# One slab earlier at the seam between attention heads and recurrent heads, and a loop turned by a stage

## What is computed

```
p = h @ w_in                       # q, k, v, z of 8 attention heads; qk, v, i, f, o, z of 4 recurrent heads
a = softmax(q1 k1) - lam * softmax(q2 k2);  o_a = a @ v
y_a = rmsnorm(o_a) * (1 - lam_init) * silu(z)
qk = silu(causal_dwconv(ml_qk))    # four taps over time, per channel
h = mlstm_chunkwise(q, k, v, i, f) # scores times decay, plus the carried state
y_b = rmsnorm(h * sigmoid(o)) * silu(z)
y = concat(y_a, y_b) @ w_out
```

## Time and profile before

| | |
|---|---|
| median of three runs | 2822.48 us (2818.57 to 2824.16) |
| span of the profiled execution | 2813.1 us |
| TensorE busy | 2699.3 us, 96% |
| VectorE, GpSimd, ScalarE busy | 1531.1, 1395.4, 1029.7 us |
| mean granted TensorE clock | 0.992 of 2.4 GHz |
| attention heads | about 862 to 1531 us |
| head norm and output of head 7 | about 1531 to 1557 us |
| first recurrent head | about 1557 to 1687 us |

### The profile page before, as it was taken

How to read it: one execution, slowest core, us unless ns; L and a number is a source line. 1 busy time by engine, 2 the same in 40 slices (tenths; PEclk the granted TensorE clock), 3 DMA queues, 4 the chain that set the end, 5 groups by cost and what they waited for, 6 DMA issues and landing times.

```text
span 2813.1 us, 39247 instructions
## 1 busy us (share of the span) xinstructions
PE 2699.3 (96%) x14076; PEld 2158.8 (77%) x14076; DVE 1531.1 (54%) x2293; ACT 1029.7 (37%) x1792; POOL 1395.4 (50%) x895
## 2 busy tenths in 40 slices
PE   6999999999989999999998999999989999999997
PEld 2588888888767777777776888888778878887885
DVE  6665544544565556656557654636475033335667
ACT  3642232232244433334333222231352165545342
POOL 0587677677743422132321334334344477877664
PEclk9999999999999999999999999999999999999999
DMA  9211111111111011001110111112132232223333
GB/s 387 98 56 52 45 53 51 52 52 53 53 63 59 25 33 34 30 30 37 37 30 15 53 53 45 52 45 60 68 113 96 91 105 90 75 82 126 123 116 137
DMA packets 67519, 202.25 MB, mean 72 GB/s; under 512 B 17620, under 2 KB 23892, under 8 KB 65256
## 3 DMA queue, kind: packets, MB, share of 16 engines
q1 hardware_dynamic: 46624, 169.46, 18.4%
q10 hardware_dynamic: 20808, 31.61, 3.3%
HBM read 171.61 MB, written 29.44 MB: 71 GB/s over the span
## 4 chain that ended last, share of the span: by engine, by line
PE 76%; POOL 7%; DVE 7%; DMA 4%; issue 3%; ACT 3%; ACTq 0%; POOLq 0%; SPq 0%; DVEq 0%
PE ps L1050 23%; PE ps L1052 22%; PE ps L1051 22%; POOL slab_lo L967 3%; DMA slab_raw<-w_in 2%; PE ps L1471 2%; PE ps L1482 1%; DVE acc L2985 1%; PE ps L1126 1%; POOL gu_lo L967 1%; DMA resid<-x_t 1%; PE ps L1234 1%; PE ps L1201 1%; POOL slab_raw L958 1%; POOL gu_s L956 1%
## 5 line engine op out<-in xcount | busy, mean ns | idle before, releaser
L736 POOL TENSOR_TENSOR slab_hi<-slab_raw,zero 128x1024 fp32r<-128x1024 f32 x103 | 199.3, 1935 | 967.6 <-PE ps L1052 878.4
L1050 PE MATMUL ps<-h_hi,slab_hi 128*128 128x512 f32 x1616 | 643.8, 398 | 12.4 <-POOL h_lo L754 5.5
L1051 PE MATMUL ps<-h_lo,slab_hi 128*128 128x512 f32 x1616 | 632.1, 391 | 0.0
L1052 PE MATMUL ps<-h_hi,slab_lo 128*128 128x512 f32 x1616 | 631.5, 391 | 0.0
L1050 PEld LDWEIGHTS ps<-h_hi,slab_hi 128*128 128x128 f32 x1616 | 304.2, 188 | 90.7 <-issue 10.0
L1052 PEld LDWEIGHTS ps<-h_hi,slab_lo 128*128 128x128 f32 x1616 | 304.2, 188 | 66.5
L1051 PEld LDWEIGHTS ps<-h_lo,slab_hi 128*128 128x128 f32 x1616 | 304.5, 188 | 59.6
L740 POOL TENSOR_TENSOR slab_lo<-slab_raw,slab_hi 128x1024 fp32r<-128x1024 f32 x103 | 252.3, 2450 | 9.7 <-DVE mean L3085 1.7
L3011 DVE SCALAR_TENSOR_TENSOR resid<-ps,mod,resid 128x512 f32<-128x512 f32 x320 | 224.7, 751 | 0.5 <-issue 0.3
L801 POOL TENSOR_TENSOR slab_lo<-slab_raw,slab_hi 128x512 fp32r<-128x512 f32 x124 | 161.8, 1313 | 43.9 <-ACT slab_hi L2087 43.2
L1052 PE MATMUL ps<-t_hi,slab_lo 128*128 128x512 f32 x368 | 143.9, 391 | 0.0
(11 more groups left out here) (466 smaller groups left out, 5950.1 us busy)
## 6 DMA issues: line engine op xcount, KB each, us to landing
slab_raw<-w_in SPq DMA_DIRECT2D x168, 512.0 KB, 3.6
mod_big<-mod_w SPq DMA_DIRECT2D x12, 2048.0 KB, 12.2
slab_raw<-w_c SPq DMA_DIRECT2D x43, 512.0 KB, 3.6
res_scr<-resid ACTq DMA_DIRECT2D x4, 2048.0 KB, 7.2
resid<-res_scr ACTq DMA_DIRECT2D x2, 4096.0 KB, 12.9
gv_scr<-sg_t ACTq DMA_DIRECT2D x4, 2048.0 KB, 7.0
slab_raw<-gv_scr SPq DMA_DIRECT2D x16, 512.0 KB, 3.4
uz_scr<-gu_out SPq DMA_DIRECT2D x16, 512.0 KB, 4.8
```

The costliest lines, as they stand in the source:

```text
L736: pool.tensor_tensor(hi, raw[slot][:], zeros, ALU.add).then_inc(hi_done.sem, 1)
L1050: pe.matmul(dst, w_h, r_h, start=first, stop=False, skip_group_check=True)
L1051: pe.matmul(dst, w_h, r_l, start=False, stop=False, skip_group_check=True)
L1052: return pe.matmul(dst, w_l, r_h, start=False, stop=last, skip_group_check=True)
```

## The change

Four things, all in the order of instructions; no DMA and no instruction of GpSimd or SyncE is touched.

1. The slab IN_ML + 1 (keys) is projected by halves in the last attention head, in the steps of tiles 4 and 5, where an ordinary head projects Q. The fills of tiles 5 and 6 go, the one of tile 7 stays. ScalarE copies each half from PSUM to a new tile `x_first`, which lies over `da_qh`; TensorE waits for each copy (`a_v`) before it writes that half of the bank again.
2. The keys' convolution reads `x_first` and writes `p_0[0]`. Its first step stands in VectorE's last head, in the step of tile 7 ahead of the turn's low part; steps 1 and 2 stand between the last head and `da_gate`; the last one stands, behind the fourth step of the queries, ahead of `add_out`. The queries' third step stays ahead of the results.
3. The slab IN_ML + 2 takes the four quarters in the head norm. Before the loop over recurrent heads TensorE does the projection of IN_ML + 3 (keys turned between its halves), the scores and the turn of the first values.
4. The loop over recurrent heads has the start of head h + 1 (`ml_start`) at its end in place of that of head h at its beginning. VectorE's `ml_qk` is cut into functions, and for the first head they come in another order: low parts, weighed queries, decays, weighed keys, low parts of both. ScalarE does the high part of the weighed queries ahead of the exponential there.

```diff
@@ TensorE, last head @@
-                    if last and i >= 5:
+                    if last and i == 7:
                         keep_running(PS[3][:, half_of(1 - da_halves(tiles[0])[0])], C, 12)
...
+                    if last and i in (5, 6):
+                        pe.wait_ge(a_v.sem, a_v.at(h + 2, i - 5))
...
-                    if not last and i != 6:
+                    if i in (4, 5) or i == 7 and not last:
...
             da_values(DA_HEADS - 1, KT // 2 - 1)
-            project_quarter(IN_ML + 1, 1, 0)
+            project_quarter(IN_ML + 2, 0, 0)
             da_squares(DA_HEADS - 1, last=True)
-            project_quarter(IN_ML + 1, 1, 1)
+            project_quarter(IN_ML + 2, 0, 1)
             da_spread(DA_HEADS - 1, last=True)
             for part in (2, 3):
-                project_quarter(IN_ML + 1, 1, part)
+                project_quarter(IN_ML + 2, 0, part)
...
+            def ml_start(h):
+                n = IN_ML + 8 * h + 2
+                pe.wait_ge(m_conv.sem, m_conv.at(h, 3))
+                project(n, 0, between=lambda: turn_keys(h))
+                ml_scores(h)
+                pe.wait_ge(m_conv.sem, m_conv.at(h, 7))
+                project(n + 1, 1, between=lambda: turn_values(h, 0))
...
+            project(IN_ML + 3, 1, between=lambda: turn_keys(0))
+            ml_scores(0)
+            turn_values(0, 0)
             with pe.Fori(0, ML_HEADS - 1) as h:
                 ml_head(h)
                 ml_out(h, (nothing, nothing), IN_ML + 8 * h + 9)
+                ml_start(h + 1)
             ml_head(ML_HEADS - 1, last=True)
@@ ScalarE @@
+            def next_half(e):
+                half_done(DA_HEADS, DA_Q_SLAB, e)
+                act.wait_ge(a_score.sem, a_score.at(DA_HEADS - 1, (7, 15)[e]))
+                act.activation(x_first[:, half_of(e)], PS[3][:, half_of(e)], ACT.Copy).then_inc(a_v.sem, 1)
...
+                if first:
+                    act.wait_ge(m_q.sem, m_q.at(h))
+                    act.activation(mi_hi[:], mt[:], ACT.Copy).then_inc(m_qkh.sem, 1)
                 act.wait_ge(m_dt.sem, m_dt.at(h))
                 act.activation(decay_t[:], decay_t[:], ACT.Exp, scale=-1.0).then_inc(m_de.sem, 1)
@@ VectorE @@
+                        if last and i == 7:
+                            dve.wait_ge(a_v.sem, a_v.at(h + 2))
+                            first_keys(0)
...
             da_head(DA_HEADS - 1, last=True)
+            for j in (1, 2):
+                first_keys(j)
             da_gate(DA_HEADS - 1, 1)
...
+            def ml_qk_first():
+                value_ends()
+                queries_low(0)
+                keys_low(0)
+                dve.wait_ge(m_ld.sem, m_ld.at(0))
+                weigh_queries(0)
+                decays(0)
+                weigh_keys(0)
+                weighed_queries_low(0)
+                weighed_keys_low(0)
...
+            first_queries(3)
+            first_keys(3)
             add_out(C_DA + DA_HEADS - 1, OUT_DA + DA_HEADS - 1)
-            dve.wait_ge(in_mm.sem, in_mm.at(IN_ML + 1))
-            for j in range(CONV):
-                conv_step(0, 1, j)
-            ml_qk(0)
+            ml_qk_first()
```

More of the change, by code:

```diff
@@ L371, in build @@
         ml_so = take("ml_so", [P, NC, ML_V], at=o_v)[0]
+        x_first = take("ml_x1", [P, T], at=resid_base)[0]
         ml_z = [take(f"ml_z{b}", [P, T], at=o_w + 4 * T * b)[0] for b in range(2)]
@@ L1647, in ml_head @@
                 mm.then_inc(m_s.sem, 1)
+            def ml_start(h):
[3 more added lines that the diff above has]
+                ml_scores(h)
                 pe.wait_ge(m_conv.sem, m_conv.at(h, 7))
-                project(n + 1, 1, between=lambda: turn_values(0))
+                project(n + 1, 1, between=lambda: turn_values(h, 0))
+            def ml_head(h, last=False):
+                n, cn = IN_ML + 8 * h + 2, C_ML + 2 * h
                 pe.wait_ge(m_vl.sem, m_vl.at(h, 3))
                 project_quarter(n + 2, 0, 0)
-                turn_values(1)
+                turn_values(h, 1)
                 project_quarter(n + 2, 0, 1)
@@ L2319, in da_head @@
                         da_turned(h, i, 0)
-                    if i == 6 and not last:
-                        da_q_half(h + 1, 1)
+                    if i == 6:
+                        next_half(1) if last else da_q_half(h + 1, 1)
                     if i + 1 < KT:
@@ L2330, in da_head @@
                         da_turned(h, i, 1)
-                    if not last and i == 4:
-                        da_q_half(h + 1, 0)
                     if i == 4:
+                        next_half(0) if last else da_q_half(h + 1, 0)
                         da_square(h, 0)
@@ L2387, in _, with ml_queries @@
                 da_high(DA_HEADS - 1, e)
-            def ml_queries(h):
-                act.wait_ge(m_conv.sem, m_conv.at(h, 3))
+            def ml_queries(h, first=False):
+                act.wait_ge(m_conv.sem, m_conv.at(h, 6 if first else 3))
                 act.activation(mt[:], mt[:], ACT.Silu).then_inc(m_silu.sem, 1)
@@ L2416, in ml_qk @@
                 act.activation(kw_hi[:].rearrange("p c k -> p (c k)"), xp[:, 0:T], ACT.Copy).then_inc(m_kwh.sem, 1)
-                act.wait_ge(m_q.sem, m_q.at(h))
-                act.activation(mi_hi[:], mt[:], ACT.Copy).then_inc(m_qkh.sem, 1)
+                if not first:
+                    act.wait_ge(m_q.sem, m_q.at(h))
+                    act.activation(mi_hi[:], mt[:], ACT.Copy).then_inc(m_qkh.sem, 1)
             def ml_gate(h, e):
@@ L3228, in da_result_low, with conv_step, first_queries, first_keys @@
                    .then_inc(a_yl.sem, 1)
+            def conv_step(h, which, j, source=None, into=None, event=None):
+                dst, x = (mt, kt)[which] if into is None else into, PS[which] if source is None else source
+                event = 4 * which + j if event is None else event
+                col = lambda tap: par[:, bass.ds(h + (COL["conv_w"] + 8 * tap + 4 * which), 1)]
+                if j == 0:
+                    dve.tensor_scalar(dst[:], x, col(CONV - 1), par[:, bass.ds(h + (COL["conv_b"] + 4 * which), 1)],
+                                      ALU.mult, ALU.add).then_inc(m_conv.sem, 1)
+                else:
+                    dve.wait_ge(m_conv.sem, m_conv.at(h, event - 1))
+                    dve.scalar_tensor_tensor(dst[:, j:T], x[:, 0:T - j], col(CONV - 1 - j), dst[:, j:T], ALU.mult, ALU.add)\
+                       .then_inc(m_conv.sem, 1)
+            def first_queries(j):
+                conv_step(0, 0, j, v_t[:], event=3 + j)
+            def first_keys(j):
+                conv_step(0, 1, j, x_first[:], p_0[0], event=7 if j == CONV - 1 else j)
             def da_head(h, first=False, last=False):
@@ L3330, in ml_qk, with decays @@
                 dve.memset(va_lo[:, :, ML_V:VA].bitcast(F32), 0.0).then_inc(m_vl.sem, 1)
-                dve.wait_ge(m_ld.sem, m_ld.at(h))
+            def decays(h):
                 for c in range(NC):
@@ L3340, in ml_qk, with keys_low, weigh_keys @@
                    .then_inc(m_qkl.sem, 1)
+            def keys_low(h):
                 dve.wait_ge(m_qkh.sem, m_qkh.at(h, 1))
                 dve.tensor_tensor(mk_lo[:], kt[:], mk_hi[:].bitcast(F32), ALU.subtract).then_inc(m_qkl.sem, 1)
+            def weigh_keys(h):
                 dve.wait_ge(m_ktr.sem, m_ktr.at(h))
@@ L3427, in _ @@
             CONV_AFTER = (0, 2, 4, 6, 8, 10, 12, 14)
-            dve.wait_ge(a_v.sem, a_v.at(DA_HEADS))
             for j in range(2):
-                conv_step(0, 0, j, v_t[:])
+                first_queries(j)
             da_norm(DA_HEADS - 1)
-            for j in range(2, CONV):
-                conv_step(0, 0, j, v_t[:])
+            first_queries(2)
             for e in range(2):
```

51 lines of the change are left out of this document (26 added, 25 removed).

## The result

The changed kernel takes 2827.66 us (median of ten runs, 2819.49 to 2834.23); the kernel before, run beside it, 2817.94 (ten runs, 2813.4 to 2824.16). The recorded ratio, which is not the quotient of the two medians (that is 1.0034), is 1.0028, with a 95% interval from 1.0017 to 1.0038: slower by some 7.9 us (4.8 to 10.7). The time lies inside the forecast's range, and 2.2 us from its figure, but the median of three from which the sum was made was itself 4.5 too high. Against the measured ratio the + 3.1 is too small. "Within 0.2%" was called the likeliest case; the ratio lies above it, though the interval's lower end, 0.17%, does not exclude it.

A forecast was written before the change was run, and what follows sets the result against it. TensorE was taken as the bound, busy 2699.3 of 2813.1 us. Terms + 2.0 - 1.5 + 4.2 + 2.2 - 5.9 + 2.1 = + 3.1 us on the median 2822.48 gave 2825.5, range 2818.5 to 2830.5.

The forecast's parts named there:

- Within 0.2%: Whole kernel: time within 5.6 us of the kernel before, given a chance of 0.66.
- last head (with its half clock): Last attention head: half slabs in place of fills cost + 2.0 us, the full clock returning gives - 1.5.
- norm: wait, turns, half clock: Head norm: waiting for slab IN_ML + 2 delays the output projection + 4.2 us, slow clock behind adds + 2.2.
- start of the first recurrent head: Output projection's end to first quarter of IN_ML + 4: + 23.2 in place of + 29.1, a gain of 5.9 us.
- half clock in the quarter: First quarter of IN_ML + 4: 1.2 GHz clock after the waits in the head's start costs + 2.1 us.
- the first key step: Last attention head, ahead of VectorE's turn of tile 7: takes 0.55 us, costs nothing, 0.5 at most.
- the full clock at this place: Tile-7 fill of the last attention head: full clock instead of 1.2 GHz gives 1.5 us, bounds 0 to 1.6.
- A: Norm and head start: new waits bring no costly half clock; sum - 1.2 us, 2821; chance 0.20.
- B: Norm and head start: VectorE and GpSimd hardly meet, slabs ready early, clock stays; 2818 or 2815 us; chance 0.15.
- C: Last output half of head 6 to IN_ML + 4: GpSimd's queue bounds both ends, half clock; + 8.2, 2830.7; chance 0.13.
- D: Last attention head: a copy or convolution step lands in the softmax chain; + 1 to + 3 more, 2827 to 2829; chance 0.09.
- E: Head norm: the third slab isn't in the norm's shade, its split bound to the last output half; part of the forecast.

The follow-up runs named there:

- e6: Changed kernel with key step 1 moved behind the queries' step 1 and key step 2 behind the result's low parts; 2819.59 us, 1.0012.
- e4: e3 with, for the first recurrent head, the split of IN_ML + 4 also ahead of the causal product; 2817.32 us, 0.9991.
- e5: Changed kernel with 19 and 21 matmuls that nobody reads put into TensorE's two new waits; 2816.92 us, 0.9998.
- e9: The kernel before, unaltered, measured as if it were a changed one; 2817.94 us, 1.0008.
- e11: One more profile of the kernel before, unaltered, one run; 2811.72 us.
- e3: Changed kernel with GpSimd's split of IN_ML + 2 ahead of that of head 7's output slab; 2819.51 us, 0.9999.
- e8: e4 with the key steps moved as in e6 and 13 fills in the wait ahead of IN_ML + 4; 2818.70 us, 1.0001.
- e2: Kernel before with only the loop over recurrent heads turned by a stage; 2820.35 us, 0.9999.
- e12: One more profile of the changed kernel, unaltered, one run; 2824.43 us.
- e10: The changed kernel a third time, unaltered; 2825.51 us, 1.0031.
- e7: Changed kernel with IN_ML + 2 projected whole behind the output projection, none in the norm, keys still in the last head; 2821.70 us, 1.0014.

## Why the prediction was right, and where it was not

**The stretch, by its own steps**, with means of three and four profiles:
```
step                                forecast   measured
last head (with its half clock)     + 0.5      + 0.96   (36.32 -> 37.28)
norm: wait, turns, half clock       + 6.4      + 5.97   (13.79 -> 19.76)
start of the first recurrent head   - 5.9      - 6.17   (29.06 -> 22.89)
half clock in the quarter           + 2.1      + 2.55   ( 2.73 ->  5.28)
sum                                 + 3.1      + 3.3    (93.1  -> 96.4)
```
The steps behind it held too. The slab came 4.75 to 4.77 after the last values (5.0); GpSimd's two passes had 1.0 and 0.8 us of turns and the key steps 1.6 each (1.1 each for both sides), and e6 takes the turns away alone and lands at 2.9 (3.1). The Trainium skill, SBUF — State Buffer, section Who interferes with whom, states that a VectorE instruction with two SBUF inputs contends with a GpSimd instruction that reads SBUF. The trace agrees, with 1.09 us from the end of GpSimd's pass to the end of VectorE's step, in the earlier trace rows and again in the changed kernel, and with e6's bare 1.89 and 2.34. One reading was wrong without harm: the first key step was put at 0.55 us, from a row in which it ran beside GpSimd, and took 0.80 in the last head, where VectorE waited 1.53 us behind it. In the start the causal product began 13.9 behind the output projection (14.3), and product and split took 8.8 us together, as summed, though in another way: the product 3.53, the passes 2.87 and 2.34. The gain was 6.2 and not the 11 of the projection, and e4 shows what stood behind the split: VectorE's low part of the values, 1.8 sooner.

**The clock.** That each new wait has a half clock behind it was right in all four profiles of the changed kernel, and e5 shows both by their absence. The term that was mis-sized is the clock's in the last head, "the full clock at this place, which gives 1.5 us". It was read from one profile as if it belonged to the tile-7 fill. That fill took 4.50 in the profile before, but 2.92 in both e9 and e11, where the half clock lies elsewhere in the same head, behind another of its waits. Windows of e11:
```profile
1505.00:1510.00 5.00, 3.12 (x14) 2.24 (x12) 3.69 (x7) 2.37 (x5) 0.00 (x0) 1.00 0.00 0
1510.00:1515.00 5.00, 4.76 (x28) 4.41 (x30) 1.02 (x3) 0.60 (x1) 0.00 (x0) 0.67 0.00 0
```
The old head has it once in each of three profiles, at three places, and takes 36.1 to 36.5 each time. The changed head has none in two profiles (36.57) and one at the fill in two (37.98; 4.08 and 3.99 for the fill). With the other experiments that keep this last head (e3 to e8), five profiles of ten have it and five have none. So the gain was there by halves: 0.7 on average in place of 1.5, within the bounds of 0 to 1.6. The work put into the head was costed well: 36.57 without a half clock is 1.8 us more than the 34.8 that the old head would take without its own (an estimate, 36.3 less 1.5), and the forecast was 2.0.

**The rest of the time.** The three comparisons of the changed kernel give 1.0028, 1.0029 and 1.0031, near 8 us; the stretch explains 3.3. By the second table the spans differ by 9.4 on average (2813.3 and 2822.7): seam 3.5, ahead of the seam 2.2, the last recurrent head's end 1.2, the gate stage 2.5. The part ahead of the seam scatters by 7 us in the kernel before and by 5 in the changed one, and nothing that is changed runs there. The granted clock accounts for it. Cut the trace into pieces of 10 us, and take of each its length times what its granted clock lacks to 1.00; ahead of the seam these sum up to 10.3, 15.3 and 8.6 us in the three profiles before and 17.0, 12.0, 13.6 and 11.9 in the four after. The stage less this sum is 1456.8 to 1457.8 us in all seven. So the 2.2 us are stretches at the half clock, of which the profiles of the changed kernel happen to have more. In the seam the same sum is 1.7 in each profile before and 6.8 to 7.0 in each one after. At the end of the last recurrent head two of the three profiles before have the full clock (1.00 over 2020 to 2050), and all four of the changed kernel have a stretch at the half clock there (0.89 to 0.94, as has e2 with 0.89 and the first profile before with 0.94). The long gate stage of e12 is half clock as well (the sum there is 5.1, and 0 in the other six), but the 526.9 and 526.8 of the first two profiles after are not. There TensorE waits for `slab_lo` a little more often. One line of the table of waits, the profile before and then the first after (us in total, times, longest):
```profile
PE ps L1050 <- POOL slab_lo L967: 1.6, 2, 0.9
```
```profile
PE ps L1051 <- POOL slab_lo L968: 3.7, 5, 1.0
```
But e11 has 2.9 in four such waits and a stage of 524.1, and e10, the changed kernel, 1.7 in two and 523.5, the shortest of all. So the level isn't fixed by the kernel's order, and the few profiles can't say whether the change makes the long form more frequent.
Set beside the times, the stretch does better than that suggests. All against the kernel before, in us:
```
          e2     e3     e4     e5     e6     e7     e8     changed
stretch  -0.5   -2.5   -3.4   -0.2   +1.0   +4.5   -3.4   +3.3
time     -0.3   -0.3   -2.5   -0.6   +3.4   +3.9   +0.3   +7.9, +8.2, +8.7
```
Each time has an interval of about 3 us to either side. Six kernels agree with their stretch within it; e8 misses by 3.7, and the changed kernel by 5 in all three comparisons. These 5 us have no shown cause. The gate stage alone is not it: e5, e7 and e8 show it at 526.3 to 526.7 in their profiles as well. The clocks recorded with the runs narrow it down. Their mean is 0.9886 over 29 executions of the changed kernel, 0.9913 over 100 of the kernel before, and 0.9914 over the 12 of e5. The difference is 0.0027, or 7.7 us of the span, of which the seam has 5.2; among the executions recorded at 0.989 and at 0.990 the changed kernel is only 2.2 and 2.5 us slower. So some of the 5 us go with more half clock outside the seam, and why there is more of it there stays open. What is shown is the sign and the main mechanism: with GpSimd's order put right (e3) or the waits filled (e5) the kernel is level with the one before.

**The rivals.** A, no half clock, is refuted by every profile of the changed kernel. B, the projection really saved, is refuted in the order as written: IN_ML + 4 was ready at + 22.7, where it decided from + 21. e4 reaches + 21.0 and has the early slab in the norm, and there the kernel does come out 2.5 us faster. C wanted the half clock at 1520 to stay and the splits to take over 2 us longer than bare: the first held in two profiles of four, the second nearly (1.8). Its sum of + 8.2 is what was measured as time, but by number alone: its terms for the norm (8.1) and the start (- 4.5) were not found (5.97, - 6.17), and the stretch gives 3.3. D's copies and steps cost nothing seen: TensorE waited 0.78 and 0.97 behind the scores of tile 7 where it waited 1.82 before. E was part of the forecast, and held.

**The base.** The forecast in us is near the truth by luck, because two errors met: a base 4.5 too high and a sum 5 too low. Given as a ratio, it was 1.0011 against 1.0028. The 9.4 us between span and median were put down to what lies around the span. The runs that have both figures show 1.7 to 1.8 us for that (a few of e5 more). The other 7.6 were scatter between a fast profiled execution and a median of three.

## What to carry to other kernels

A step moved forward on one engine is only as early as its input in the queue of the engine that prepares it: read that queue, and move the preparation too (e3 was worth 8 us in time, 5.8 of them in the stretch). A wait of 3 to 5 us in front of a burst of matmuls costs its length and then 1.7 to 2.6 us more in a half clock behind it, unless something is run in it (e5). Which of several short waits is followed by the half clock changes from one execution to the next (five profiles of ten have it in the new last head), so a term read from a single profile needs a second one before it is put into a sum.

## What the runs showed of the hardware that was not expected

- The half clock wanders among waits of about 2 us. Behind the same wait of 2.1, ahead of the values in the step of tile 6, the granted clock was 1.00 in the profile before (1511 to 1516) and 0.67 in e11 (1510 to 1515). In front of a whole quarter and behind 2.92 us or more (e6, e4's 3.50, 4.75, 5.3) it came every time.
- It costs no less behind a shorter wait: the quarter, from its start to the next work, took 5.4 us behind 2.92 (e6), 5.3 behind 3.50 (e4), 4.5 to 4.9 behind 4.75 to 4.77 (the changed kernel's first quarter), and behind 5.3 it took 5.3 in the changed kernel and 4.5 to 4.6 in e3 and e6, against 2.7 to 2.9 at full speed. So a wait shorter by 1.8 us gave 0.8.
- VectorE's reciprocal, with one input in memory, is not lengthened beside a pass of GpSimd: 1.74 us beside one in e7, 1.75 with GpSimd idle in the changed kernel. The multiply-add steps with two inputs went from 1.28 to 2.8. One input in memory is not the whole distinction: the multiply step that opens a convolution (TENSOR_SCALAR, one input) took 0.80 alone and 2.16 to 2.75 beside passes.
- A kernel on one core scatters by 13 us from run to run (2813 to 2826 in 31 runs of the kernel before), and for the greater part this goes with the granted clock. Over the 100 runs with a recorded clock the slow ones have the low clocks (correlation - 0.76), and ahead of the seam the profiles differ by up to 8 us with the half clock counted and by 1 without it.
